# Expert gates of a dense PEER layer: summed per cell and scattered through DRAM instead of multiplied out from one-hot rows

## The reference

```python
q = einsum('bsd,de->bse', x, wq).reshape(B, S, 8, 2, 128)
s1 = einsum('bshc,kc->bshk', q[..., 0, :], keys1); s2 = ... (q[..., 1, :], keys2)
v1, i1 = top_k(s1, 16); v2, i2 = top_k(s2, 16)
cand = v1[..., :, None] + v2[..., None, :]            # 16 x 16 per token and head
vals, pos = top_k(cand, 16); ids = (i1 * 128 + i2) at pos
gates = softmax(vals)
h = einsum('td,tkd->tk', x, u_tab[ids])               # 128 picks per token
out = einsum('tk,tkd->td', gelu(h) * gates, v_tab[ids])
```

## Time and profile before

| | |
|---|---|
| median of 3 runs | 2414.81 us (2414.21 to 2416.8) |
| the profiled execution | 2416.51 us |
| its span, first to last instruction | 2414.8 us |
| mean granted clock of TensorE | 0.982 |
| busy: PE / DVE / ACT / POOL | 96% / 64% / 43% / 3% |
| moved by DMA | 425.28 MB |

### The profile page before, as it was taken

How to read it: one execution, slowest core, us unless ns; L and a number is a source line. 1 busy time by engine, 2 the same in 40 slices (tenths; PEclk the granted TensorE clock), 3 DMA queues, 4 the chain that set the end, 5 groups by cost and what they waited for, 6 DMA issues and landing times.

```text
span 2414.8 us, 45807 instructions
## 1 busy us (share of the span) xinstructions
PE 2307.8 (96%) x15504; PEld 2135.9 (88%) x15504; DVE 1538.1 (64%) x2726; ACT 1028.5 (43%) x1390; POOL 72.5 (3%) x64
## 2 busy tenths in 40 slices
PE   4999999899899989999999999999999999999996
PEld 4999999897699879999999999999788888888885
DVE  4446655565653568777779898989555555555556
ACT  2444455554444443444443333333444444444442
POOL 0000000000010040000000000000000000000000
PEclk9999999999999999999999999999999999999998
DMA  6655555455544555555554445444566666666663
GB/s 178 189 182 164 172 178 168 155 181 177 192 142 156 187 166 172 182 182 182 181 177 131 160 157 159 157 157 157 182 193 194 202 205 201 201 202 202 206 193 123
DMA packets 116576, 425.28 MB, mean 176 GB/s; under 512 B 13840, under 2 KB 13856, under 8 KB 115520
## 3 DMA queue, kind: packets, MB, share of 16 engines
q1 hardware_dynamic: 112608, 412.14, 54.1%
q0 software_dynamic: 3936, 12.71, 2.2%
HBM read 418.50 MB, written 6.29 MB: 176 GB/s over the span
## 4 chain that ended last, share of the span: by engine, by line
PE 90%; DVE 5%; DMA 3%; issue 1%; ACT 1%; DVEq 0%; SPq 0%; ACTq 0%
PE ps L1212 24%; PE ps L1199 17%; PE ps L1194 17%; PE ps L1195 17%; PE ps L1219 12%; PE ps L1448 2%; DMA raw<-in_w_in 2%; DVE w_lo L720 1%; DMA ln_gb<-in_ln_in 1%; DVE bn L733 0%; DVE x L739 0%; DVE tk_ab L1022 0%; PE ps L1320 0%; PE ps L1390 0%; DVE x L745 0%
## 5 line engine op out<-in xcount | busy, mean ns | idle before, releaser
L720 DVE TENSOR_TENSOR w_lo<-raw,w_hi 128x1024 fp32r<-128x1024 f32 x774 | 957.7, 1239 | 713.7 <-PE ps L1219 418.0
L436 ACT ACTIVATE w_hi<-raw 128x1024 fp32r<-128x1024 f32 x774 | 820.5, 1061 | 1061.2 <-DMA raw<-in_peer_v 384.2
L1194 PE MATMUL ps<-x_t_hi,w_hi 128*128 128x256 f32 x3328 | 835.9, 289 | 21.0 <-ACT v_t L486 12.5
L1195 PE MATMUL ps<-x_t_lo,w_hi 128*128 128x256 f32 x3328 | 820.9, 284 | 0.0
L1194 PEld LDWEIGHTS ps<-x_t_hi,w_hi 128*128 128x128 f32 x3328 | 641.7, 193 | 25.9 <-ACT w_hi L436 15.9
L1195 PEld LDWEIGHTS ps<-x_t_lo,w_hi 128*128 128x128 f32 x3328 | 642.4, 193 | 0.0
L1199 PE MATMUL ps<-x_t_hi,w_lo 128*128 128x256 f32 x3328 | 472.1, 285 | 13.5 <-DVE w_lo L720 13.5
L1199 PEld LDWEIGHTS ps<-x_t_hi,w_lo 128*128 128x128 f32 x3328 | 433.3, 194 | 14.8 <-DVE w_lo L720 14.7
L1212 PE MATMUL ps<-w_hi,x_t_hi 128*128 128x512 f32 x1024 | 315.8, 390 | 3.0 <-DVE x_t_lo L1131 3.0
L1212 PE MATMUL ps<-w_hi,x_t_lo 128*128 128x512 f32 x1024 | 316.1, 390 | 0.0
L1219 PE MATMUL ps<-w_lo,x_t_hi 128*128 128x512 f32 x1024 | 274.1, 389 | 0.0
(11 more groups left out here) (204 smaller groups left out, 1313.8 us busy)
## 6 DMA issues: line engine op xcount, KB each, us to landing
raw<-in_u SPq DMA_DIRECT2D x256, 512.0 KB, 4.6
raw<-in_peer_v SPq DMA_DIRECT2D x256, 512.0 KB, 4.9
raw<-in_w_in SPq DMA_DIRECT2D x128, 512.0 KB, 4.6
raw<-in_branch SPq DMA_DIRECT2D x32, 512.0 KB, 3.9
raw<-in_wout SPq DMA_DIRECT2D x32, 512.0 KB, 3.7
raw<-in_wq SPq DMA_DIRECT2D x32, 512.0 KB, 3.8
raw<-in_pleg SPq DMA_DIRECT2D x32, 512.0 KB, 3.8
x<-in_x SPq DMA_DIRECT2D x2, 1024.0 KB, 6.2
```

What stands on the lines that cost most here:

```text
L436: nc.scalar.activation(HI[:, u % 4, :], RAW[:, u % 4, :], ACT.Copy).then_inc(hi_ready, 1)
L720: v.tensor_tensor(LO[:, u % 2, :], RAW[:, u % 4, :], HI[:, u % 4, :].bitcast(F32), ALU.subtract) \
L1194: mm(o, w(HI, u % 4)[:, k, :], xh[:, ks * half + k, :], start=(s and k == 0), stop=False)
L1195: mm(o, w(HI, u % 4)[:, k, :], xl[:, ks * half + k, :], start=False, stop=False)
```

## The change

The one-hot products are gone. Units 0 to 255 of phase u all run as the first half did. The gates take another way:

- The search runs on both token halves together, in 16 steps a head, one after each `conv`, from unit 7 of phase wq on: 128 steps, 25 beside wq, 32 beside pleg, the rest beside units 0 to 6 and 27 to 91 of u. wq, pleg and u are written out on DVE instead of looped.
- A cell's number is i2 * 16384 + i1 * 128 + token. The softmax is done for heads 0 to 2 and then for 3 to 7 (`gates_in`, `gates_out`, ACT `exp_gates`).
- `merge_gates` sums gates that fall on the same cell: for each pick one scalar_tensor_tensor over the token's row of cells with an accumulated result, five after each `conv`, beside units 7 to 26 (96 of them, 48 columns) and 105 to 136 (160 of them, 128 columns).
- POOL zeroes a 16.8 MB table in DRAM with 16 DMAs after phase v, scatters the sums with 256 indirect DMAs of 128 single words (96 in the first batch, 160 in the second), and then reads the table back by chunks, two DMAs of 64 KB a chunk into three slots.
- `gated` multiplies a chunk of `experts` by its gates on DVE (128 x 256), two after each `conv` from unit 191 on.
- ACT loads two more activation tables; it waits for the scatter before unit 224, where the sums' buffer is reused. The second table is multiplied as before.

```diff
-TOPK_CHUNKS = 64
-FIRST_ONES = 104
+BATCHES = ((0, 3), (3, 8))
+G_SLOTS = 3
+G_FROM = 190
...
             pool.wait_ge(rel_out, 16)
+            pool.wait_ge(zero_ready, 1)
+            pool.wait_ge(unit_done, BASE["qk"])
+            for n in range(16):
+                pool.dma_start(gates_dram[n // 8][n % 8 * 16:n % 8 * 16 + 16].rearrange("k p e -> p k e"), ZERO[:, :, :]
+                               ).then_inc(zero_out, 16)
...
-            pool.wait_ge(spill_out, 32)
-            nc.gpsimd.memset(BUF[:, TOPK_CHUNKS:FIRST_ONES, :], 1.0).then_inc(ones_ready, 1)
-            pool.wait_ge(picks_sb, 1)
-            nc.gpsimd.memset(BUF[:, FIRST_ONES:NK, :], 1.0).then_inc(ones_ready, 1)
+            pool.wait_ge(zero_out, 16 * 16)
+            for h0, h1 in BATCHES:
+                for h in range(h0, h1):
+                    pool.wait_ge(gates_ready, h + 1)
+                    for tt in range(NT):
+                        if h:
+                            pool.wait_ge(scattered[tt], 16 * TOPK * h)
+                        for p in range(TOPK * h, TOPK * (h + 1)):
+                            pool.indirect_dma_start(out=cells[tt], out_offset=bass.IndirectOffsetOnAxis(
+                                ap=ID[:, tt, p:p + 1], axis=0), in_=GSC[:, tt, p:p + 1], in_offset=None
+                                ).then_inc(scattered[tt], 16)
+            for tt in range(NT):
+                pool.wait_ge(scattered[tt], 16 * PICKS)
+            for k in range(NK):
+                if k >= G_SLOTS:
+                    pool.wait_ge(g_mult, k - G_SLOTS + 1)
+                for tt in range(NT):
+                    pool.dma_start(GR[:, k % G_SLOTS, tt * P:(tt + 1) * P], gates_dram[tt][k]
+                                   ).then_inc(g_in[k % G_SLOTS], 16)
...
             def pool_sums(g):
-                dve.wait_ge(const_ready, 3)
+                dve.wait_ge(const_ready, 4)
+                dve.wait_ge(zero_out, 16 * 16)
...
+            def merge_gates(b, n):
+                h0, h1 = BATCHES[b]
+                ch.wait()
...
+                for m in range(NT * TOPK * h0 + 5 * n, min(NT * TOPK * h0 + 5 * n + 5, NT * TOPK * h1)):
+                    h, tt, p = m // (NT * TOPK), m // TOPK % NT, m // (NT * TOPK) * TOPK + m % TOPK
+                    width = TOPK * h1
+                    ins = v.scalar_tensor_tensor(out=SAME[:, m % 5, 0:width], in0=IDF[:, tt, 0:width],
+                                                 scalar=IDF[:, tt, p:p + 1], in1=GATE[:, tt, 0:width],
+                                                 op0=ALU.is_equal, op1=ALU.mult, accum_out=GSC[:, tt, p:p + 1])
...
+            def gated(k):
+                dve.wait_ge(act_evac, 80 + k + 1)
+                dve.wait_ge(g_in[k % G_SLOTS], 16 * NT * (k // G_SLOTS + 1))
+                v.tensor_tensor(BUF[:, k, :], BUF[:, k, :], GR[:, k % G_SLOTS, :], ALU.mult).then_inc(g_mult, 1)
...
+            for n in range(32):
+                if n % 2 == 0:
+                    st(None, n // 2)
+                conv(None, 4, BASE["pleg"] + n + DVE_LEAD)
+                search(25 + n)
+            done, found = 0, 57
+            for n in range(2 * NK):
+                conv(None, 4, BASE["u"] + n + DVE_LEAD)
+                if n == 6:
+                    gates_out(0)
+                if n == 104:
+                    gates_out(1)
+                if 7 <= n < 27:
+                    merge_gates(0, n - 7)
+                elif 105 <= n < 137:
+                    merge_gates(1, n - 105)
+                elif found <= STAGES * HEADS:
+                    search(found)
+                    found += 1
+                while done < min((n - G_FROM) * 2, n // 2 - 2):
+                    gated(done)
+                    done += 1
+            for k in range(done, NK):
+                gated(k)
...
-            with pe.Fori(0, 16) as i:
+            with pe.Fori(0, 32) as i:
...
-            def gate_products(i, j):
...
-            b_unit(None, 0)
-            b_unit(None, 1)
-            turn_picks()
...
-            pe.wait_ge(g_used, 64)
+            pe.wait_ge(act_evac, 80 + NK)
```

More of the change, by code:

```diff
@@ L207, in hybrid_block_kernel @@
         spill = nc.dram_tensor("residual_dram", [NT, P, D], F32, kind="Internal").ap()
+        gates_dram = [nc.dram_tensor(f"gates_dram{tt}", [NK, P, P], F32, kind="Internal").ap() for tt in range(NT)]
         raw_in = [sem(f"raw_in{s}") for s in range(4)]
@@ new lines, in _, with tk0, tk1 @@
+            scores = lambda h, tt, f: SC[:, 2 * h + tt, f, :]
+            first = lambda h: slice(TOPK * h, TOPK * h + 8)
+            second = lambda h: slice(TOPK * h + 8, TOPK * (h + 1))
+            def tk0(h):
+                dve.wait_ge(peer_sb, h + 1)
+                for tt, f in each:
+                    ch.tag(v.max(V16[:, tt, f, 0:8], scores(h, tt, f)))
+                settle()
+            def tk1(h):
+                for tt, f in each:
+                    ch.tag(v.max_index(IU[:, tt, f, 0:8], V16[:, tt, f, 0:8], scores(h, tt, f)))
@@ L995, in tk2, with tk6, tk7, tk8 @@
+            def tk6(h):
+                for tt in range(NT):
+                    ch.tag(v.max(GATE[:, tt, first(h)], flat(CAND, tt)))
                 settle()
-                for f in range(2):
-                    ch.tag(v.max_index(IU[:, f, 8:16], V16[:, f, 8:16], S12[:, f, :]))
+            def tk7(h):
+                for tt in range(NT):
+                    ch.tag(v.max_index(POS[:, tt, 0:8], GATE[:, tt, first(h)], flat(CAND, tt)))
+            def tk8(h):
+                for tt in range(NT):
+                    ch.tag(v.match_replace(flat(CAND2, tt), GATE[:, tt, first(h)], flat(CAND, tt), LOWEST))
@@ L998, in tk2, with tk9, tk10 @@
                 settle()
[L1000 to L1003 removed]
+            def tk9(h):
+                for tt in range(NT):
+                    ch.tag(v.max(GATE[:, tt, second(h)], flat(CAND2, tt)))
                 settle()
[L1005 removed]
+            def tk10(h):
+                for tt in range(NT):
+                    ch.tag(v.max_index(POS[:, tt, 8:16], GATE[:, tt, second(h)], flat(CAND2, tt)))
@@ L1101, in _ @@
-            dve.wait_ge(act_evac, 80 + TOPK_CHUNKS)
-            onehots(None, 0)
-            onehots(None, 1)
-            conv(None, 4, ub + 3)
-            onehots(None, 2)
-            spread(None, 0)
-            conv(None, 4, ub + 4)
-            onehots(None, 3)
-            onehots(None, 4)
-            spread(None, 1)
-            def u_body(i, last):
-                for j in range(4):
-                    if not (last and j == 3):
-                        onehots(i, j + 1)
-                    conv(i, 4, ub + j + DVE_LEAD)
-                    if j % 2:
-                        spread(i, j // 2)
@@ new lines, in gates_out @@
+            def gates_out(b):
+                h0, h1 = BATCHES[b]
+                dve.wait_ge(ge_exp, b + 1)
+                for tt in range(NT):
+                    g = GATE[:, tt, TOPK * h0:TOPK * h1].rearrange("p (h r) -> p h r", r=TOPK)
+                    total = GSUM[:, 8 * tt + h0:8 * tt + h1]
+                    ch.link(v.tensor_reduce(total, g, AX.X, ALU.add))
+                    ch.link(v.reciprocal(total, total))
+                    ins = v.tensor_tensor(g, g, total.unsqueeze(2).to_broadcast([P, h1 - h0, TOPK]), ALU.mult)
+                    if tt == 0:
+                        ch.tag(ins)
+                ch.link(ins)
@@ new lines, in _ @@
+            st = stage("pleg", KD + 2, gt_block, AH, AL)
+            for n in range(32):
+                conv(None, 4, BASE["wq"] + n + DVE_LEAD)
+                search(n - 7)
+            for n in range(32):
+                if n % 2 == 0:
[19 more added lines that the diff above has]
+                    done += 1
```

296 lines of the change are left out of this document (117 added, 179 removed).

## The result

| | before | after |
|---|---|---|
| median | 2415.81 us (2414.21 to 2418.31, 4 runs) | 2627.8 us (2616.54 to 2634.77, 4 runs) |
| the profiled execution | 2416.51 us | 2623.94 us |
| its span | 2414.8 us | 2622.3 us |
| mean granted clock | 0.982 | 0.934 |

Ratio 1.0872, 95% interval 1.0829 to 1.0915: slower by 212 us, where 2351 us was forecast. Lines of the changed kernel: DVE's `conv` is L744, PE's products of phase u are L1245, L1246 (with `w_hi`) and L1250 (with `w_lo`), of the second table L1263 and L1270; the indirect DMA is L432, the readback L441, `gated` L1146, the sums L1126.

A forecast was written before the change was run, and what follows sets the result against it. PE, busy 96% of the span, was taken as the bound; 69.8 us of gains less 1.3 (pleg) and 3 (zeroing) gave 65.5 us off 2416.51, so 2351 us, range 2341 to 2398 (forecast's own 2341 to 2358).

The forecast's parts named there:

- gains 1 to 4: Phase u: faster second-half units 56.2 us, join of halves 7.4, POOL's memset gone 5.4, phase-end wait for `a_lo` 0.8.
- Search, pleg, merges: DVE beside wq, pleg and u: search and merges hidden under 2.88 us a unit; pleg costs 1.3 us, 0 to 8.
- Zeroing: 16 DMAs of 1 MB between phase v and the pool phase: 3 us for late loads, 0 to 48.
- Rival C: Zeroing holds up the loads or the pool phase: 12 to 45 us more, 2363 to 2396 us; chance 0.11.
- an indirect DMA at 1.1 us, limit 1.42: Scatter on POOL beside phase u: 1.1 us taken per indirect DMA, late only past 1.42 us, so no loss.
- rival B: Scatter late, units 111 to 191, 160 x (t - 1.42): 2476 us, 2424 by mutual exclusion with `conv`; chance 0.19.
- 52 us of slack: POOL's second scatter batch: 176 us at 1.1 us each, against 228 us until the first gated chunk is due.
- Batch one is 96 with 98 units to go in: hidden: POOL's first scatter batch, 96 indirect DMAs beside 98 units of phase u, costs no time.
- the rule against it: Compute on POOL shuts DVE out, a direct issue does not; which kind an indirect issue is, no row tells.
- Readback: Table read back by chunks into three slots: PE never late up to landings of about 3.0 us; taken as 0.
- Rival A: Readback feeds too slowly: landings of 4.0 us cost 32 us for 125 chunks, 2383 us; chance 0.12.
- Rival D: Units 128 to 255 stay near 3.3 us because DVE or the DMA engines are full: 2415 us; chance 0.04.

The follow-up runs named there:

- the run that neither starves nor lacks slots: The changed kernel with one gates table, one 128 KB readback DMA a chunk and five slots instead of three, on chip 14: 2356.2 us.
- the direct run: The changed kernel with its 256 indirect DMAs replaced by direct DMAs of 128 single words each, on chip 13: 2378.24 us.

## Why the prediction was wrong

- *What bounds, and gains 1 to 4 (69.8 us).* Right as far as the runs separate them: 2.88 us a unit outside the three stretches, 2356.2 us in the run that neither starves nor lacks slots, of which 9 us are POOL's lateness (below). The forecast of 2351 left the scatter and the readback at nothing.
- *Search, pleg, merges.* Right, within the range. The run without a scatter lost nothing beside the merges. The 32 units of pleg took 98.0 us against 95.2 before (98.0 to 99.6 in the other runs), 2.9 us where 1.3 was said and 8 allowed. A 128-column sum is 0.35 us long and the next one starts 0.27 us after it, where 0.25 was said; the read of its accumulated output, 0.08 us, which no row of before could show, fits into that step.
- *Zeroing (3 us, at worst 48).* It cost 0: the first pool sum came at 200.08 us (200.30 before), with 16 landings of 17.6 us overlapping. Rival C did not come.
- *POOL: an indirect DMA at 1.1 us, limit 1.42.* The step that failed, twice over. Its size: it takes 0.96 us plus 0.30 to the next, 1.26 alone. Where DVE works, every second one takes 1.31 (the chip 14 rows above) while the `conv` beside it keeps its 1.23 us; the last five of batch two on chip 14, with DVE idle, all took 0.96. Batch two there went from 1210.03 to 1445.81 us, 1.48 us each with the waits between its rows, which by the prediction's own formula is 160 x 0.06 = 10 us too late. DVE stood 11.25 us for the first chunk of gates, and PE's units behind were 9 us late: rival B's lateness was real, at 9 us instead of 73 to 125, and of the mutual exclusion only the half that costs POOL. The rule of the Trainium skill ("SBUF — State Buffer", "Who interferes with whom") is so borne out in part: an indirect issue and a `conv` do meet, but here only POOL pays (1.31 us for 0.96), where beside POOL's compute the `conv` paid (4.19 us for 1.23). Its cover: "52 us of slack" and "Batch one is 96 with 98 units to go in: hidden" weigh POOL's deadline alone, and the rule against it weighed DVE; nothing asked whether PE keeps its pace beside an indirect DMA. The row taken for that, a direct issue beside a `conv`, speaks of direct DMAs alone, and the direct run shows that it was right for them. No row of before holds an indirect DMA, so the bound had to be open upwards there, and was not: the price is 238 to 258 us on four of five chips (13, 8, 5 and 11; for chip 13 against its own run without a scatter, for the others against 2356.2), 0.93 to 1.0 us of PE for each. The price is shown; by what way POOL's indirect DMAs hold PE and its reports stays open.
- *Readback (0, landings up to 3.0 us allowed).* The mechanism and the threshold were right, and the size of the landing was off: 3.2 us as median, not the 2.1 of the earlier trace rows. Rival A had 32 us for landings of 4.0; five slots gave back 30.8.
- *Rival D.* Wrong: the pace in units 128 to 191 outside the scatter is 2.88.
- *The chances.* Rival B had 0.19 by lateness; the starving was in no case. That the sign could turn by another road than the deadline was left out.

## What to carry to other kernels

An instruction that no row of the trace shows has two prices: its own time, and what it does to engines that share nothing visible with it. Bound the second from above too, and look for it in the idle column as "issue" in the middle of a unit of work, where no semaphore can be the reason, and as "remote" on the engines that wait for it. Tie rows of indirect DMAs one by one to the progress of the engine that sets the pace, so that a stall stops its cause; singly at one per unit it cost nothing here. And an experiment that heals something needs its unhealed control on the same chip: here the same kernel stands 10% apart from chip to chip while the kernel before stands still.

## What the runs showed of the hardware

- Indirect DMAs issued every 1.26 us bring PE nearly to a stand (58 products in 40 us instead of 333), and it recovers when they stop. The first stall came 8 to 16 us after the first of a row of them, 22 us beside the second table and once, in a second batch, 38 us. It happened on four chips of five, in every run there that had such rows. It doesn't depend on the places written, on the number of offsets (32 or 128), on PE's loop, or on the phase; direct DMAs twice as dense do nothing. One per 2.88 us costs PE nothing.
- Semaphore raises are late or missing in the same stretches, PE's by up to 62 us: 34 to 157 of the 2322 reports in each of the fourteen kernels that starve or are paced on those chips, none in the kernel before, in the run without a scatter and the one with direct DMAs, and one at most in each of the three on chip 14.
- What lies between POOL's issue and PE's instructions isn't settled. No transfer queued up: in the changed kernel the first packet of an indirect DMA stands 1.5 to 4.0 us behind its issue, and the 32nd of the first row has 1.56 us like the 12th. All executions were profiled ones. Raises that are missing from the record in just these stretches make it plausible that the recording has a part in the stall, but no run without the profiler was made. Why one chip is free of it is open.
